# First feed-forward product by seven half products in place of eight, in feature groups of 512, with the residual sums in DRAM

## What is computed

```python
x = x + m @ w_o
h = rmsnorm(x, norm_mlp)
x = x + jnp.square(jax.nn.relu(h @ w_ff1)) @ w_ff2
```

## Time and profile before

| | us |
|---|---|
| median of 3 runs | 1681.88 (1680.07 to 1683.41) |
| the profiled execution, whole | 1683.65 |
| its span from first to last instruction | 1681.9 |
| TensorE busy in the span | 1647.1 (98%) |
| VectorE busy | 687.9 (41%) |
| ScalarE busy | 483.2 (29%) |

### The profile page before, as it was taken

The page is one execution under the profiler, slowest core; times in us unless marked ns, Lnnn a source line. Parts: engine busy times, 40 slices in busy tenths (PEclk is TensorE's granted clock), DMA queues, the critical chain, the costliest instruction groups (busy, mean ns, idle before and its releaser), DMA issues. The chain is left out here.

```text
span 1681.9 us, 28428 instructions
## 1 busy us (share of the span) xinstructions
PE 1647.1 (98%) x10711; PEld 1596.5 (95%) x10711; DVE 687.9 (41%) x1236; ACT 483.2 (29%) x925; POOL 79.1 (5%) x94
## 2 busy tenths in 40 slices
PE   7999999999989999999999999999999999999997
PEld 7899999888988999999999999999999999999997
DVE  5212223334644444333654353333333333333566
ACT  5222224433534443111423320133111320133223
POOL 0160000000000000000121000000000000000021
PEclk9999999999999999999999999999999999999999
DMA  5254554332257785532111112111111111111224
GB/s 163 83 154 130 163 172 137 103 106 95 85 153 178 190 200 148 168 110 84 51 38 50 50 30 58 37 50 37 50 41 46 41 46 50 37 50 37 63 67 153
DMA packets 237202, 155.87 MB, mean 93 GB/s; under 512 B 23982, under 2 KB 227590, under 8 KB 237146
## 3 DMA queue, kind: packets, MB, share of 16 engines
q1 hardware_dynamic: 208590, 124.00, 26.2%
q10 hardware_dynamic: 26268, 28.31, 5.0%
q0 software_dynamic: 2288, 2.80, 0.7%
HBM read 122.00 MB, written 35.43 MB: 94 GB/s over the span
## 5 line engine op out<-in xcount | busy, mean ns | idle before, releaser
L647 PE MATMUL bank<-xhi,wh 128*128 128x352 f32 (+1 forms) x1104 | 372.0, 337 | 3.9 <-DVE xlo L1578 1.8
L648 PE MATMUL bank<-xlo,wh 128*128 128x352 f32 (+1 forms) x1104 | 360.2, 326 | 0.0
L649 PE MATMUL bank<-xhi,wl 128*128 128x352 f32 (+1 forms) x1104 | 359.8, 326 | 0.0
L1124 ACT ACTIVATE wh<-wr 128x1024 fp32r<-128x1024 f32 (+1 forms) x142 | 144.6, 1018 | 433.0 <-PE bank L649 332.0
L1540 DVE TENSOR_TENSOR wl<-wr,wh 128x1024 fp32r<-128x1024 f32 (+1 forms) x142 | 181.6, 1279 | 188.7 <-ACT wh L1124 187.5
L648 PE MATMUL bank<-hlo,wh 128*128 128x368 f32 (+1 forms) x768 | 251.4, 327 | 0.0
L647 PE MATMUL bank<-hhi,wh 128*128 128x368 f32 (+1 forms) x768 | 250.6, 326 | 0.3 <-DVE rel L1964 0.3
L649 PE MATMUL bank<-hhi,wl 128*128 128x368 f32 (+1 forms) x768 | 250.1, 326 | 0.0
L647 PEld LDWEIGHTS bank<-xhi,wh 128*128 128x128 f32 x1104 | 207.3, 188 | 15.5 <-issue 7.6
L648 PEld LDWEIGHTS bank<-xlo,wh 128*128 128x128 f32 x1104 | 207.6, 188 | 0.0
L649 PEld LDWEIGHTS bank<-xhi,wl 128*128 128x128 f32 x1104 | 207.5, 188 | 0.0
(11 more groups left out here) (235 smaller groups left out, 2069.1 us busy)
## 6 DMA issues: line engine op xcount, KB each, us to landing
wr<-in_w_ff_dram SPq DMA_DIRECT2D x72, 512.0 KB, 3.9
wr<-in_w_in_dram SPq DMA_DIRECT2D x46, 512.0 KB, 4.2
d_T<-stg ACTq DMA_DIRECT2D x18, 544.0 KB, 2.8
kvc<-in_cache_kv_g_dram SPq DMA_DIRECT2D x16, 512.0 KB, 6.1
kvc<-in_cache_kv_g_dram SPq DMA_DIRECT2D x32, 256.0 KB, 7.3
d_tm<-tm ACTq DMA_DIRECT2D x12, 512.0 KB, 3.7
d_m<-bb ACTq DMA_DIRECT2D x8, 544.0 KB, 3.1
ml<-d_m SPq DMA_DIRECT2D x8, 544.0 KB, 4.4
```

The costliest lines, as they stand in the source:

```text
L647: pe.matmul(bank[c][:, 0:n], wh[st_.p][:, k, :], a, start=(k == 0), stop=False)
L648: pe.matmul(bank[c][:, 0:n], wh[st_.p][:, k, :], b, start=False, stop=False)
L649: last = pe.matmul(bank[c][:, 0:n], wl[st_.p][:, k, :], a, start=False, stop=(k == nk - 1))
L1124: act.activation(wh[st_.p][:, 0:nk, :], wr[st_.p][:, 0:nk, :], ACT.Copy).then_inc(w_hi, 1)
```

## The change

The first product (up) of a group is made by Strassen's scheme, one level. The operands are cut in two along the inner features (even and odd tiles of 128), the weights along the output features (two column blocks) and the data along the tokens (two halves of 544). A pair of column blocks then takes seven half products (`unit`), each of 4 inner tiles by 544 tokens, where eight would be plain. A unit is 2 x 4 x 3 = 24 matmuls of 272 columns. The data sums T1 to T4 (`tall`) are made once, from `x2` scaled in place by the norm weight, by DVE, POOL and ACT; the weight sums (`s1`, `s2` and two more in place) are made by DVE for each pair. The very first pair is made of plain units (four double units of 48 matmuls, of the order 3 to 6) while the sums are being made. Units that feed several outputs share banks, and DVE adds products together (`add_products`, 5 for each pair); ACT then makes relu, square and high part as three dependent instructions (`chain`), DVE the rest.

There are 8 groups of 512 hidden features in place of 4 of 1024. After two pairs comes `down`, 8 column blocks over 4 tiles, in an order that begins with the first chunk of two blocks. `hall` and `tall` fill the room in which `x2` and the wide `fhi` and `flo` stood, so the residual sums are stored in DRAM (`d_x2`) and pass through a ring of four tiles (`xring`) in each group: SP loads, DVE adds, SP stores. In the last group the split weights stay in SBUF (`lh`, `ll`) for the second pass, and four residual tiles lie in `xlow`.

The core of the diff:

```diff
+NG_F, KF = 8, 4
+HALF, HT = TOK // 2, TOK // 4
...
+T_ORDER = (0, 2, 1, 3)
+DOWN_ORDER = [(0, 0), (1, 0), (0, 1), (0, 2), (1, 1), (1, 2)] + [(j, c) for j in range(2, KD) for c in range(3)]
...
-    fhi = at("fhi", [P, KD, TOK], RA, F32R)
-    flo = at("flo", [P, KD, TOK], RA + 34816, F32R)
+    tall = at("tall", [P, 4, 2, KF, HALF], RA, F32R)
+    hall = at("hall", [P, 4, 2, KF, HALF], RB, F32R)
+    xring = at("xring", [P, KF, TOK], RB + 52224)
+    xlow = at("xlow", [P, KF, TOK], RB)
+    fhi = at("fhi", [P, KF, TOK], RC, F32R)
+    flo = at("flo", [P, KF, TOK], RC + 17408, F32R)
+    lh = at("lh", [P, KD, KF, P], RA, F32R)
+    ll = at("ll", [P, KD, KF, P], RA + 16384, F32R)
...
+    d_x2 = scratch("d_x2", [KD, P, TOK])
...
+        def ring_load(g, j):
+
+            sp.wait_ge(xr_st[j % 2], g * 64 + 16 * (j // 2 + 1))
+            sp.dma_start(xring[:, j % 4, :], d_x2[(j + 4) % 8]).then_inc(xr_ld[j % 4], 16)
...
+        def down_loads(g):
+            for j in range(KD):
+                if j < 4:
+                    down_load(g, j + 4, u_lo, unit_at(g, 14 + j) + 1)
+                else:
+                    up_load(DOWN_SLOT[j - 4], g + 1, 0, u_lo, unit_at(g, 14 + j) + 1)
+                sp.wait_ge(y_d, g * 24 + DOWN_POS[(j, 2)])
+                sp.dma_start(d_x2[j], xring[:, j % 4, :]).then_inc(xr_st[j % 2], 16)
+                if j:
+                    ring_load(g, j - 1)
+            ring_load(g, KD - 1)
+
...
-        def quarter_up(q, first):
-            with pe.Fori(first, 4) as i:
-                for p in range(2):
-                    for c in range(3):
-                        chunk(Step(S_MLP + p, (16, q), (2, i)), KD, c, hhi, hlo)
...
+        def unit_products(g, l, operand, k, c, out, start, stop):
+            a, b = operand[:, 0, k, HT * c:HT * c + HT], operand[:, 1, k, HT * c:HT * c + HT]
+            p = (l - 3) % 2
+            pe.matmul(out, uh[p][:, k, :], a, start=start, stop=False, skip_group_check=True)
+            pe.matmul(out, uh[p][:, k, :], b, start=False, stop=False, skip_group_check=True)
+            return pe.matmul(out, ul[p][:, k, :], a, start=False, stop=stop, skip_group_check=True)
+
+        def unit(g, l, operand, b0, fresh=True):
+            pe.wait_ge(u_lo, unit_at(g, l) + 1)
+            for c in range(2):
+                for k in range(KF):
+                    last = unit_products(g, l, operand, k, c, banks8[:, b0 + c, 0:HT], fresh and k == 0, k == KF - 1)
+            last.then_inc(u_done, 1)
+
+        def plain_unit(l, operands, b0, fresh):
...
+        def up_pair(g, q):
+            n, l0 = pair_at(g, q), 7 * q
+            first = isinstance(g, int) and g == 0
+            bA, bB, bC, bD = (4, 6, 0, 2) if first else (0, 2, 4, 6)
+            if first:
+                pe.wait_ge(f_a, 1)
+            else:
+                pe.wait_ge(f_a, n * 8 + 5)
+                if q == 0:
...
+            unit(g, l0, hall[:, B11], bA)
+            if first:
+                pe.wait_ge(f_a, 3)
+                pe.wait_ge(h_lo, KD + 15)
+            elif q == 0:
+                pe.wait_ge(y_t, g * 24)
+            unit(g, l0 + 1, tall[:, T2], bB)
+            if first:
+                pe.wait_ge(f_a, 5)
+            else:
+                pe.wait_ge(ev, n * 5 - 1)
+            unit(g, l0 + 2, tall[:, T3], bC)
+            if first:
+                pe.wait_ge(f_a, 7)
+            else:
+                pe.wait_ge(ev, n * 5)
+            unit(g, l0 + 3, tall[:, T1], bD)
+            pe.wait_ge(h_lo, KD + 16)
+            pe.wait_ge(ev, n * 5 + 2)
+            unit(g, l0 + 4, tall[:, T4], bC, fresh=False)
+            pe.wait_ge(p1_a, n + 1)
+            unit(g, l0 + 5, hall[:, B21], bA, fresh=False)
+            pe.wait_ge(ev, n * 5 + 3)
+            unit(g, l0 + 6, hall[:, B22], bD, fresh=False)
+
+        def down(g):
+            first = isinstance(g, int) and g == 0
+            used = ((4, 5, 6), (7, 2, 3)) if first else ((0, 1, 2), (3, 4, 5))
+            for j, c in DOWN_ORDER:
+                l = 14 + j
+                p = (l - 3) % 2
+                if c == 0:
+                    pe.wait_ge(u_lo, unit_at(g, l) + 1)
...
+        pe.wait_ge(h_lo, 7)
+        plain_unit(3, (B11, B12), 4, True)
 
         pe.wait_ge(sqa_p, 8)
-        pe.wait_ge(ones_p, 1)
+        pe.wait_ge(set_p, 6)
         pe.wait_ge(res_d, 24)
         for c, (t0, n) in enumerate(CH):
-            pe.matmul(bank[3 + c][:, 0:n], ones[:], ssqa[:, t0:t0 + n], start=True, stop=True).then_inc(n2_pe, 1)
-        quarter_down(0)
-        with pe.Fori(1, 3) as q:
-            quarter_up(q, 0)
-            quarter_down(q)
-        quarter_up(3, 0)
-
-        def products(st_, src, out, split=None, ks=range(KD)):
+            pe.wait_ge(taken[c], S_MLP)
+            pe.matmul(bank[c][:, 0:n], ones[:], ssqa[:, t0:t0 + n], start=True, stop=True).then_inc(n2_pe, 1)
+        pe.wait_ge(h_lo, 8)
+        plain_unit(4, (B21, B22), 4, False)
+        pe.wait_ge(r2_d, 3)
+        plain_unit(5, (B11, B12), 0, True)
+        plain_unit(6, (B21, B22), 0, False)
+        up_pair(0, 1)
+        down(0)
+        with pe.Fori(1, NG_F - 1) as g:
+            up_pair(g, 0)
+            up_pair(g, 1)
...
+        def chain(e, parity, tile, half, src=None):
+
+            r = rel[parity]
+            if src is not None:
+                if above_zero(e - 1):
+                    act.wait_ge(f_lo, e - 1)
+                act.activation(split2(r[:]), src, ACT.Relu).then_inc(f_a, 1)
+            else:
+                act.activation(r[:], r[:], ACT.Relu).then_inc(f_a, 1)
+            act.wait_ge(f_a, e * 2 + 1)
+            act.activation(r[:], r[:], ACT.Square).then_inc(f_a, 1)
+            act.wait_ge(f_a, e * 2 + 2)
+            act.activation(chain_out(fhi, tile, half), r[:], ACT.Copy).then_inc(f_hi, 1)
+
...
+        def t_parts(n):
+            k = T_ORDER[n]
+            for o, (t, ready_sem, count) in enumerate(((tA, t_d, 3 * n + 1), (tB, t_p, n + 1), (tA, t_d, 3 * n + 2),
+                                                       (tA, t_d, 3 * n + 3))):
+                act.wait_ge(ready_sem, count)
+                act.activation(tall[:, (T3, T1, T2, T4)[o], 0, k, :], t[:], ACT.Copy).then_inc(h_hi, 1)
+
+        unit_hi(0, 4, uraw[A12], r_in[A12], 16)
+        t_parts(0)
+        act.wait_ge(x2_st[(KD - 1) % 2], 16 * KD // 2)
+        act.wait_ge(h_lo, KD)
+        act.activation(x2[:, KD - 1, :], x2[:, KD - 1, :], ACT.Copy, scale=g2c[:, KD - 1:KD]).then_inc(h_scaled, 1)
+        unit_hi(0, 5, uraw[A21], r_in[A21], 16)
+        t_parts(1)
+        unit_hi(0, 6, uraw[A22], r_in[A22], 16)
+        act.wait_ge(u_done, 2)
+        act.wait_ge(r2_d, 3)
+        chain(0, 0, 0, 0, two(4))
+        chain(1, 1, 0, 1, two(6))
+        t_parts(2)
+        up_hi(0, 1, 0)
+        t_parts(3)
...
         act.activation(rst[:, 1, 15:16], ssq[:, 15:16], ACT.Sqrt).then_inc(root_warm, 1)
-        split_hi(Step(S_FIRST + 1), KD)
+        last_hi(1)
+        chain_12(NG_F - 1, 1)
         for j in range(KD):
...
+        def t_first(n):
+            k = T_ORDER[n]
+            h1, h2 = x2[:, 2 * k, :], x2[:, 2 * k + 1, :]
+            dve.wait_ge(h_scaled, 2 * k + 2)
+            dve.wait_ge(h_lo, KD + 4 * n)
+            dve.tensor_tensor(tA[:], h2[:, HALF:TOK], h1[:, HALF:TOK], ALU.subtract).then_inc(t_d, 1)
+            t_lo_part(n, 0, tA)
+            t_lo_part(n, 1, tB)
+            dve.wait_ge(h_lo, KD + 4 * n + 1)
+            dve.tensor_tensor(tA[:], tA[:], h1[:, 0:HALF], ALU.add).then_inc(t_d, 1)
+
+        def t_second(n):
+            h2 = x2[:, 2 * T_ORDER[n] + 1, :]
+            t_lo_part(n, 2, tA)
+            dve.wait_ge(h_lo, KD + 4 * n + 3)
+            dve.tensor_tensor(tA[:], h2[:, 0:HALF], tA[:], ALU.subtract).then_inc(t_d, 1)
+
+        def t_third(n):
+            t_lo_part(n, 3, tA)
+
...
+        unit_lo(0, 4, uraw[A12])
+        t_first(0)
+        t_second(0)
+        t_third(0)
+        unit_lo(0, 5, uraw[A21])
+        mean_squares()
+        t_first(1)
+        t_second(1)
+        t_third(1)
+        unit_lo(0, 6, uraw[A22])
+        chain_lo(0, 0, 0, 0)
+        chain_lo(1, 1, 0, 1)
+        t_first(2)
+        t_second(2)
+        t_third(2)
+        up_lo(0, 1, 0)
+        sum_1(0, 1)
+        sums_23(0, 1)
+        t_first(3)
+        t_second(3)
+        t_third(3)
+        chain_lo(2, 0, 1, 0)
+        chain_lo(3, 1, 1, 1)
+        up_dve(0, 1)
+        down_dve(0)
+        with dve.Fori(1, NG_F - 1) as g:
+            up_dve(g, 0)
...
+        for n, k in enumerate(T_ORDER):
+            pool.wait_ge(h_scaled, 2 * k + 1)
+            if n:
+                pool.wait_ge(h_lo, KD + 4 * n - 2)
+            pool.tensor_tensor(tB[:], x2[:, 2 * k, HALF:TOK], x2[:, 2 * k, 0:HALF], ALU.subtract).then_inc(t_p, 1)
```

More of the change, by code:

```diff
@@ new lines, in unit @@
+        def unit(g, l, operand, b0, fresh=True):
[5 more added lines that the diff above has]
+        def plain_unit(l, operands, b0, fresh):
```

(46 more changed lines are left out.)

567 lines of the change are left out of this document (374 added, 193 removed).

## The result

| | before | after |
|---|---|---|
| median of 20 runs each, us | 1682.64 | 1680.18 (1677.69 to 1682.36) |
| ratio, 95% interval | | 0.9986 (0.998 to 0.9993) |
| span of the profiled execution | 1681.9 | 1678.5 |
| last add of the output projection starts | 898.99 | 897.22 |
| from there to the last `acc` | 772.87 | 771.25 |

A forecast was written before the change was run, and what follows sets the result against it. TensorE, busy 98% of the span, was taken to bound the kernel. Terms -35.4 + 22.1 + 2 + 1.2 + 6 + 7 - 3 gave -0.1 us on 1681.9; forecast 1683 us, range 1668 to 1702.

The forecast's parts named there:

- products: Up products on TensorE: 2712 matmuls at 126.7 ns, 343.5 us for 378.9, a gain of 35.4 us; down unchanged.
- waits of the first pair: From output projection into first pair: TensorE waits while DVE makes T1 to T4 and weight rests, +22.1 us.
- clock behind the longest: First pair, behind the 10.4 us wait: a stretch at the 1.2 GHz clock level, +2 us.
- joints, eight: End of up in each of 8 groups: down's first chunk waits for the last chain, 0.75 us each, +6 us.
- last group, first pass: Last group: wait for the second chunk's chain, then DVE held by POOL in a 5.05 us cycle, together +7 us.
- second pass: Last group's second pass: 17.0 us less, 14.1 of it already counted in down, so -3 us.
- allowance for hand-overs: Loop groups: hand-overs a little over 0.04 us (0.06 to 0.08) add 1 to 2 us over six groups.
- rival 2: Loop hand-overs of 0.16 us: joints +10 us over six groups, first pair 5 us more, 1698 us; chance 0.25.
- (1): Helpers cheaper than walked: joints close (-6), last group's DVE keeps up with TensorE (-5), 1672 us; chance 0.3.
- (3): Clock falls at the joints too: 1.7 us at each of 8, 7 in last group's gaps, 1708 us; chance 0.07.
- (4): Narrow matmuls on TensorE aren't cheaper: +54 us, 1737 us; chance 0.03.
- (5): Up: seven units don't shorten the path because DVE bounds it, some 1720 us; chance 0.02.

The follow-up runs named there:

- filler: The changed kernel with idle products of 272 columns ahead of units 5, 7 and 8 of the first pair; 1678.42 us, 0.9977 of the kernel before.

## Why the prediction was right or wrong

The measured terms, by the steps of the prediction. Each is taken from starts: what a wait costs is the distance of the two starts around it less that of the stream. They add up to -1.8, and the marks give -1.6.

| step | predicted | measured | from |
|---|---|---|---|
| products | -35.4 | -39.2 | 2712 x 125.25 ns for 378.9 us |
| waits of the first pair | +22.1 | +22.4 | unit 8 starts at 948.87, 51.65 behind the last add |
| clock behind the longest | +2 | +2.5 | 5.50 us for 3.01; 2.3 by the filler |
| reciprocals in the first down | +1.2 | +1.3 | L1199 <- `ul`, 1.48 between starts |
| joints, eight | +6 | +6.1 | 0.87 + 6 x 0.67 + 1.24 |
| last group, first pass | +7 | +5.4 | 40.01 us to the end of its last add, 67.92 before, with 33.3 us of products less |
| second pass | -3 | -1.1 | 24.64 us for 39.85, with 14.1 us of products less; 1.6 of low clock in it |
| start of down | 0 | +0.8 | 47.48 us for 47.36, seven times |

**The products were mis-sized by 3.8 us.** This is the step that failed: the term of -35.4 us was -39.2. It is the largest single error: with it put right alone the sum would have been -3.9 us in place of -0.1, and the forecast would have lain on the faster side. I drew a line through two widths and read it 48 columns outside, 126.7 ns; the up of a group runs at 125.25, and the runs of single widths show that the intervals don't lie on one line.

**The joints were right, in part by luck.** I had 0.75 us for each. In the six groups of the loop TensorE is idle for 0.51 us, but its starts stand 0.80 apart for 0.13, so a joint costs 0.67, and 0.72 came back when the order of the tiles was changed. The first and the last cost more than I had, 0.87 and 1.24, and that the eight make the 6 us is chance.

**The allowance for hand-overs was for nothing.** I had added 1 to 2 us to the point for loops in which a hand-over takes "a little over 0.04". It is as short there as in straight code. Two dependent steps of ACT in a loop group, in order of time:

```profile
1330.40 0.66 ACT L1666 ACTIVATE rel<-rel 128x544 f32<-128x544 f32 x1
1331.09 0.66 ACT L1668 ACTIVATE fhi<-rel 128x544 fp32r<-128x544 f32 x1
```

0.69 us from start to start for 0.66 of work. The row that I had read as 0.16 was one of an `acc` whose reader had its wait in an instruction of its own; rival 2, at a chance of 0.25, rested on that row and is out.

**The last group was right in its mechanism and 1.6 us too dear.** A cycle is 4.80 us, not 5.05, and the second chunk waits 1.52, not 2.1. I had blamed the root table's load for that wait; moved away, it gives back 0.49 only. The pauses of TensorE in a block are 0.3 us where I had about 0.9.

**The first pair was right** in its sum (51.1 predicted, 51.65 measured) and its single waits (3.6, 2.3, 5.3 and 10.4 predicted before units 5 to 8). Measured were 3.88, none above 0.2, 5.42 and 7.86, since part of unit 5 and nearly all of unit 7 ran at low clock, which filled the waits behind them.

**The second pass** gained 1.1 instead of 3 us. Of the 1.9 missing 1.6 are there because the 2.17 us wait ahead of it was followed by low clock in this execution; in others it wasn't (below).

Taken together: the mechanisms and places hold but for the root table's load, and the large ones have an experiment of their own; the reciprocals, the start of down and the second pass are read from traces alone. Large terms of both signs left a sum near zero whose sign was set by the 2 to 4 us errors in them. The chances of 0.32, 0.31 and 0.37 said as much; the point itself was 2.8 us too high, by the products, the first pass and the allowance for hand-overs, less what the second pass, the start of down and the clock cost more. That it missed by no more than that is luck, since these errors partly cancel. Of the other rivals none came: TensorE's gaps stayed in the last group (1), the clock didn't fall at the joints of the changed kernel (3), narrow products are cheaper (4), and DVE leaves no unit waiting in the loop (5).

## What to carry to other kernels

A scheme that saves products on the engine that bounds must have its preparation laid beside work that needs none of it: here the first pair, beside which DVE made all four sums, took back 20 of the 39 us, and with 3.0 us of plain products more there the stretch got 17.5 shorter. Where a product starts behind a chain of dependent steps, let it use last the operand that is ready last: here it took no more work and removed the joints of the loop, 0.7 us each, while in the first group the wait only moved on to a weight rest. And size the largest term by a row of the width that the change will have; a term sized by a line read outside its points was off by more than the whole result.
